# Head norms, group norm and mixing in the accumulation banks, and another order of transposes, in the attention stage of a three-block kernel

## The reference, cut to what matters

```
xn = rmsnorm(x, norm_attn);  proj = xn @ w_in            # 1024 -> 6656 columns
rq, rk, rv, rg, sq, sk, sv, ga, gb = split(proj)         # 512 512 1024 1024 512 512 512 1024 1024
rq = rope(rmsnorm(rq by 8 heads of 64, g));  rk = rope(rmsnorm(rk by heads, g)) / 8
ret = retention(rq, rk, rv)      # 8 heads of 128, two chunks of 128 tokens, decayed causal scores
ret = group_norm(ret by head, g) * silu(rg);   y_a = ret @ w_branch_ret
sq, sk = rmsnorm by heads;       sb = stick_breaking(sq, sk, sv);   y_b = sb @ w_branch_sb
x = x + (sigmoid(ga) * y_a + sigmoid(gb) * y_b) @ w_out
x = x + peer(rmsnorm(x, norm_ffn), ...)                  # and the two blocks after it
```

## Time and profile before

| | us |
|---|---|
| median of three executions | 1872.47 |
| the profiled execution's own time | 1876.42 |
| its span, first to last instruction | 1874.6 |
| busy TensorE, whole span | 1787.5 (95%) |
| busy VectorE, ScalarE, GpSimd | 1036.0, 884.3, 1089.4 |
| attention stage, up to the transposes of the next norm | 0 to about 293 |

### The profile page before, as it was taken

One profiled execution on the slowest core, in us unless ns is written; L12 is line 12 of the kernel. 1 busy time (PEld: TensorE's weight loads), 2 busy tenths in 40 slices (PEclk: granted clock), 3 DMA queues, 4 the chain that ended last, 5 costly groups with the idle time before them and its releaser, 6 DMA issues. The chain is left out here.

```text
span 1874.6 us, 36082 instructions
## 1 busy us (share of the span) xinstructions
PE 1787.5 (95%) x14238; PEld 1627.0 (87%) x14238; DVE 1036.0 (55%) x1756; ACT 884.3 (47%) x1200; POOL 1089.4 (58%) x431
## 2 busy tenths in 40 slices
PE   8799779999999999999999998999998999989998
PEld 6688669999999999888888887899997889979997
DVE  5953541597437878644444443354338863564443
ACT  5246424345543333354455455465447742345544
POOL 7764556588876666545554566565556530556563
PEclk9899889999999999999999999999999999999999
DMA  7433235255554444456567643355543411034542
GB/s 298 157 135 119 92 128 219 74 182 185 175 165 137 144 134 145 135 192 194 195 196 264 237 154 124 135 203 202 191 159 120 158 24 71 27 135 181 202 176 82
DMA packets 66178, 292.67 MB, mean 156 GB/s; under 512 B 12960, under 2 KB 13344, under 8 KB 47904
## 3 DMA queue, kind: packets, MB, share of 16 engines
q1 hardware_dynamic: 66080, 291.27, 44.6%
HBM read 289.14 MB, written 1.05 MB: 155 GB/s over the span
## 5 line engine op out<-in xcount | busy, mean ns | idle before, releaser
L2607 POOL TENSOR_TENSOR unit_lo<-unit_raw,unit_hi 128x2048 fp32r<-128x2048 f32 (+1 forms) x86 | 343.1, 4013 | 188.3 <-ACT unit_hi L1512 175.6
L2622 POOL TENSOR_TENSOR rows_lo<-rows_raw,rows_hi 128x1024 fp32r<-128x1024 f32 x128 | 308.0, 2408 | 136.7 <-ACT rows_hi L1618 85.2
L2628 POOL TENSOR_TENSOR a_lo<-table,a_hi 128x256 fp32r<-128x256 f32 x128 | 178.8, 1397 | 168.4 <-ACT a_hi L1642 168.4
L2260 DVE TENSOR_TENSOR rows_lo<-rows_raw,rows_hi 128x1024 fp32r<-128x1024 f32 x128 | 162.0, 1266 | 188.2 <-ACT rows_hi L1637 188.2
L776 PE MATMUL bank<-x_hi,rows_hi 128*128 128x256 f32 x1024 | 256.2, 288 | 1.7 <-ACT rows_hi L1600 1.7
L777 PE MATMUL bank<-x_lo,rows_hi 128*128 128x256 f32 x1024 | 250.7, 283 | 0.0
L1637 ACT ACTIVATE rows_hi<-rows_raw 128x1024 fp32r<-128x1024 f32 x128 | 135.6, 1060 | 171.0 <-PE bank L837 171.0
L2655 POOL TENSOR_TENSOR up_lo<-up_raw,up_hi 128x2048 fp32r<-128x2048 f32 x22 | 111.1, 5052 | 156.5 <-ACT up_hi L1694 126.4
L776 PEld LDWEIGHTS bank<-x_hi,rows_hi 128*128 128x128 f32 x1024 | 195.8, 191 | 1.9 <-issue 1.9
L1512 ACT ACTIVATE unit_hi<-unit_raw 128x2048 fp32r<-128x2048 f32 x71 | 135.6, 1917 | 130.8 <-PE bank L569 101.3
L777 PEld LDWEIGHTS bank<-x_lo,rows_hi 128*128 128x128 f32 x1024 | 196.1, 192 | 0.0
(11 more groups left out here) (453 smaller groups left out, 3971.0 us busy)
## 6 DMA issues: line engine op xcount, KB each, us to landing
unit_raw<-in_ring SPq DMA_DIRECT2D x75, 1024.0 KB, 4.8
rows_raw<-in_u SPq DMA_DIRECT2D x128, 512.0 KB, 3.6
rows_raw<-in_v SPq DMA_DIRECT2D x128, 512.0 KB, 4.2
up_raw<-in_up SPq DMA_DIRECT2D x44, 1024.0 KB, 5.3
down_raw<-in_down SPq DMA_DIRECT2D x22, 1024.0 KB, 4.9
const<-in_const SPq DMA_DIRECT2D x1, 1792.0 KB, 14.3
X<-in_x SPq DMA_DIRECT2D x2, 512.0 KB, 4.1
unit_raw<-in_ring SPq DMA_DIRECT2D x4, 256.0 KB, 5.4
```

The source lines that it names most:

```text
L2260: V.tensor_tensor(rows_lo[q][:, :], rows_raw[q][:, :], rows_hi_f[q % 2], ALU.subtract).then_inc(S("v_lo_ready"), 1)
L2607: return nc.gpsimd.tensor_tensor(unit_lo[SLOT_OF[n]][:, w], unit_raw[SLOT_OF[n]][:, w], hi, ALU.subtract)
L2622: nc.gpsimd.tensor_tensor(rows_lo[q][:, :], rows_raw[q][:, :], rows_hi_f[q % 2], ALU.subtract).then_inc(S("u_lo_ready"), 1)
L2628: nc.gpsimd.tensor_tensor(a_lo[q % 2][:, :], table[:, i * ROWS_RING + q, :], a_hi_f[q % 2], ALU.subtract).then_inc(S("a_lo_ready"), 1)
```

## The change

The diff below is cut: removed lines that stand in the kernel above are left out, as are the declarations. TensorE's block comes first, then ScalarE's, then VectorE's.

For slices 0, 1, 4 and 5 ScalarE now squares both banks into `tmp` and VectorE sums them. The square root takes its scale and its epsilon in the same instruction. VectorE scales, multiplies by the gain and rotates within the banks, group of tokens by group of tokens, and only the last operation writes `proj`; with it the bank is drained. ScalarE copies slices 2, 3 and 6. The group norm is made by pair of heads (`centred`, `rows_squared`, `scaled_and_gated`) while the values stand in their `ry` banks, and these banks are held out of the ring meanwhile; `ry` is drained by the last multiplication. The transposes of `Y` follow pair by pair (`retention_turned`) after slices 10, 11 and 12 and once more behind the last values of stick breaking, and `ret_hi`, `ret_lo` have a place of their own. The Sigmoid of slice 12 moves behind the last `retention_hi` on ScalarE. The mixing multiplies in the `yb` bank. Of the last transposes two banks are filled between the token groups of the second `yb`, the other two between the halves of the first `wo`.

```diff
-    ret_hi, ret_lo = x_hi, x_lo_attn
+    ret_hi, ret_lo = (view(n, ARENA_AT + TC * PROJ_W + KT * SEQ * i, [KT, SEQ], F32R) for i, n in enumerate(("ret_hi", "ret_lo")))
+    ret_junk = view("ret_junk", XN_AT + 1536, [4, DV])
...
-                        mm(outs[c][:, :], at_(x_hi_, k, c), hi[:, k, :], start=False, stop=False)
+                        mm(outs[c][:, :], at_(x_hi_, k, c), hi[:, k, :], start=half == 0 and k == 0, stop=False)
...
+                    if between and halves == 1 and c == 0:
+                        between()
...
+    def retention_turned(b):
+        o = fill(("rt", b))
+        for j in range(4):
+            h, c = 2 * b + j // 2, j % 2
+            wait_drained(pe, ("ry", h))
+            t = nc.tensor.transpose(o[:, j * P:(j + 1) * P], Y[:, c, h * DV:(h + 1) * DV], ident)
+        full(("rt", b), t)
+    def mixed_turned(banks):
+        for b in banks:
+            o = fill(("mt", b))
+            for j in range(4):
+                k, c = 2 * b + j // 2, j % 2
+                wait_drained(pe, ("yb", b // 2, c))
+                t = nc.tensor.transpose(o[:, j * P:(j + 1) * P], Y[:, c, k * P:(k + 1) * P], ident)
+            full(("mt", b), t)
...
             ret_values(2 * j - 16)
             ret_values(2 * j - 15)
+            plan.hold([("ry", h) for h in range(max(0, 2 * j - 18), 2 * j - 14)])
+        if j == N_WIN - 1:
+            plan.hold([])
...
+        if 8 <= j <= 11:
+            plan.hold([("ry", 2 * j - 16), ("ry", 2 * j - 15)])
...
+        if j >= 10:
+            retention_turned(j - 10)
...
+    retention_turned(3)
...
+        rows("ya", UNIT_AT["BRET"] + 2 * j, j, ret_hi, ret_lo, arrived=None if j else lambda k: wait_drained(pe, ("rt", k // 2)))
     for half in range(2):
         wait_drained(pe, ("sb", half))
...
+    rows("yb", UNIT_AT["BSB"], 0, sb_hi, sb_lo, halves=1)
+    rows("yb", UNIT_AT["BSB"] + 1, 1, sb_hi, sb_lo, halves=1, tokens_last=True, between=lambda: mixed_turned((0, 1)))
+    rows("wo", UNIT_AT["WOUT"], 0, mix_hi, mix_lo, arrived=lambda k: wait_drained(pe, ("mt", k // 2)), between=lambda: mixed_turned((2, 3)))
+    rows("wo", UNIT_AT["WOUT"] + 2, 1, mix_hi, mix_lo, tokens_last=True)
...
+    def gated(j):
+        for c in range(TC):
+            o = wait_filled(act, ("proj", j, c))
+            drain(("proj", j, c), A(proj[:, c, j * 512:(j + 1) * 512], o[:, :], ACT.Silu if j < 9 else ACT.Sigmoid))
+    def rows_squared(p):
+        for n in range(2):
+            h = 2 * p + n
+            act.wait_ge(S("ret_centred"), h + 1)
+            o = PS[plan.at[("ry", h)][0]]
+            for c in range(TC):
+                at_ = 400 + 2 * h + c
+                A(ret_junk[:, 2 * n + c, :], o[:, c * DV:(c + 1) * DV], ACT.Square, accum_out=stat[:, at_:at_ + 1]).then_inc(S("ret_squared"), 1)
+        act.wait_ge(S("ret_squared"), 4 * p + 4)
+        w = slice(416 + 4 * p, 420 + 4 * p)
+        A(stat[:, w], stat[:, 400 + 4 * p:404 + 4 * p], ACT.Sqrt, scale=1.0 / DV, bias=eps).then_inc(S("ret_sd"), 1)
+    def retention_hi(b):
+        hi_of(("rt", b), ret_hi[:, 2 * b:2 * b + 2, :], ("ret_group_norm", 2 * b))
...
+        if upto >= 2 and j in (0, 1, 4, 5):
+            s = (0, 1, 4, 5).index(j)
+            if s:
+                act.wait_ge(S("qk_ms"), s)
+            for c in range(TC):
+                o = wait_filled(act, ("proj", j, c))
+                A(tmp[:, 0, c * 512:(c + 1) * 512], o[:, :], ACT.Square).then_inc(S("qk_squared"), 1)
+        elif j < 7:
+            for c in range(TC):
+                copy(("proj", j, c), proj[:, c, j * 512:(j + 1) * 512])
         if upto >= 2 or 2 * j + 4 < UNIT_AT["BRET"]:
             units_ahead(2 * j + 4)
...
+        if upto >= 2 and j in (0, 1, 4, 5):
+            act.wait_ge(S("qk_ms"), s + 1)
+            A(stat[:, 128 + 16 * s:144 + 16 * s], stat[:, 64 + 16 * s:80 + 16 * s], ACT.Sqrt, scale=1.0 / DK, bias=eps).then_inc(S("qk_sd"), 1)
+        if 7 <= j < N_WIN - 1 or upto < 2 and j >= 7:
+            gated(j)
...
+        if 8 <= j <= 11:
+            rows_squared(j - 8)
+        if j >= 10:
+            retention_hi(j - 10)
...
+    retention_hi(3)
     hi_of(("sb", 1), sb_hi[:, 2:4, :])
...
+    gated(N_WIN - 1)
+    units_ahead(UNIT_AT["WOUT"] + 1)
     for b in range(4):
         hi_of(("mt", b), mix_hi[:, 2 * b:2 * b + 2, :])
+        if b == 1:
+            units_ahead(UNIT_AT["WOUT"] + 2)
...
+        j, at_ = (0, 1, 4, 5)[s], (RQ, RK, SQ, SK)[s]
+        ve.wait_ge(S("qk_squared"), 2 * s + 2)
+        sums = stat[:, 64 + 16 * s:80 + 16 * s]
+        V.tensor_reduce(sums, tmp[:, 0, :].rearrange("p (g d) -> p g d", d=DK), AX, ALU.add).then_inc(S("qk_ms"), 1)
         ve.wait_ge(S("qk_sd"), s + 1)
         rs = stat[:, 192 + 16 * s:208 + 16 * s]
...
+        step(V.reciprocal(rs, stat[:, 128 + 16 * s:144 + 16 * s]))
+        x = [wait_filled(ve, ("proj", j, c))[:, :].rearrange("p (h d) -> p h d", h=HEADS) for c in range(TC)]
+        y = [proj[:, c, at_:at_ + 512].rearrange("p (h d) -> p h d", h=HEADS) for c in range(TC)]
+        gain = bc(qk_gain[:, s, :].unsqueeze(1), [HEADS, DK])
+        for c in range(TC):
+            step.mark(V.tensor_tensor(x[c], x[c], bc(rs[:, c * HEADS:(c + 1) * HEADS].unsqueeze(2), [HEADS, DK]), ALU.mult))
+        step.sync()
         if s >= 2:
...
+            for c in range(TC):
+                drain(("proj", j, c), V.tensor_tensor(y[c], x[c], gain, ALU.mult))
             return
...
+        for c in range(TC):
+            step.mark(V.tensor_tensor(x[c], x[c], gain, ALU.mult))
+        step.sync()
         half = DK // 2
...
+        first, second = slice(0, half), slice(half, DK)
+        wave = lambda t, c: bc(t[:, c, :].unsqueeze(1), [HEADS, half])
+        part = lambda c, n: tmp[:, 1, c * 512 + n * 256:c * 512 + (n + 1) * 256].rearrange("p (h f) -> p h f", h=HEADS)
+        for n, t in enumerate((cos, sin)):
+            for c in range(TC):
+                step.mark(V.tensor_tensor(part(c, n), x[c][:, :, first], wave(t, c), ALU.mult))
         step.sync()
...
         for c in range(TC):
...
+            step.mark(V.tensor_tensor(x[c][:, :, first], x[c][:, :, second], wave(sin, c), ALU.mult))
+        step.sync()
+        for c in range(TC):
+            step.mark(V.tensor_tensor(x[c][:, :, second], x[c][:, :, second], wave(cos, c), ALU.mult))
+        for c in range(TC):
+            step.mark(V.tensor_tensor(y[c][:, :, first], part(c, 0), x[c][:, :, first], ALU.subtract))
+        step.sync()
+        for c in range(TC):
+            drain(("proj", j, c), V.tensor_tensor(y[c][:, :, second], part(c, 1), x[c][:, :, second], ALU.add))
+    if upto >= 2:
+        for s in range(4):
+            head_norm(s)
...
+    def centred(p):
+        sums = lambda h: stat[:, 384 + 2 * h:386 + 2 * h]
+        rows_of = lambda h: wait_filled(ve, ("ry", h))[:, 0:SEQ].rearrange("p (c e) -> p c e", c=TC)
+        for h in (2 * p, 2 * p + 1):
+            step.mark(V.tensor_reduce(sums(h), rows_of(h), AX, ALU.add))
+        step.sync()
+        for h in (2 * p, 2 * p + 1):
+            y = rows_of(h)
+            V.scalar_tensor_tensor(y, bc(sums(h).unsqueeze(2), [TC, DV]), -1.0 / DV, y, ALU.mult, ALU.add).then_inc(S("ret_centred"), 1)
+    def scaled_and_gated(p):
+        ve.wait_ge(S("ret_sd"), p + 1)
+        step(V.reciprocal(stat[:, 448 + 4 * p:452 + 4 * p], stat[:, 416 + 4 * p:420 + 4 * p]))
+        for h in (2 * p, 2 * p + 1):
+            o = wait_filled(ve, ("ry", h))
+            for c in range(TC):
+                wait_drained(ve, ("proj", 7 + h // 4, c))
+                w = slice(h * DV, (h + 1) * DV)
+                t = V.scalar_tensor_tensor(Y[:, c, w], o[:, c * DV:(c + 1) * DV], stat[:, 448 + 2 * h + c:449 + 2 * h + c],
+                                           proj[:, c, RG + h * DV:RG + (h + 1) * DV], ALU.mult, ALU.mult)
+            drain(("ry", h), t)
+    def retention_lo(b):
+        two = slice(2 * b, 2 * b + 2)
+        lo_of(("rt", b), ret_lo[:, two, :], ret_hi[:, two, :], ("ret_group_norm", 2 * b))
     for n in range(4):
         decayed(2 * n)
         decayed(2 * n + 1)
         if n == 1:
             stick_logits(0)
+            centred(0)
         if n == 2:
+            scaled_and_gated(0)
             stick_weights(0)
+            centred(1)
         if n == 3:
+            scaled_and_gated(1)
             stick_out(0)
             stick_logits(1)
+            centred(2)
+    scaled_and_gated(2)
+    retention_lo(0)
...
     stick_weights(1)
...
+    centred(3)
+    scaled_and_gated(3)
+    for b in (1, 2, 3):
+        retention_lo(b)
     stick_out(1)
...
+    def mixed_lo(b):
         two = slice(2 * b, 2 * b + 2)
...
+        lo_of(("mt", b), mix_lo[:, two, :], mix_hi[:, two, :])
+    gates = lambda at_, c, j: proj[:, c, at_ + j * 512:at_ + (j + 1) * 512]
+    half_rows = lambda c, j: Y[:, c, j * 512:(j + 1) * 512]
     for j in range(2):
         for c in range(TC):
+            wait_drained(ve, ("proj", 9 + j, c))
```

(49 more changed lines are left out.)

81 lines of the change are left out of this document (3 added, 78 removed).

## The result

The changed kernel took 1851.66 us (median of four executions, 1851.37 to 1853.2) against 1874.38 for the kernel before in the same session (1870.76 to 1879.43, four). The ratio is 0.9882, interval [0.9867, 0.9898], so 19 to 25 us less. A second session, 1849.44 against 1875.17, gave 0.9866 [0.9846, 0.9887]. The forecast was 1852.5 with a range of 1833 to 1865. The time was met, in part by luck: by the traces the stage gained 27 us where the sum said 20, and the median of 1872.5 that it was taken from lay 1.5 to 2.9 us under the later medians of the same kernel.

The account below looks back on a forecast made before the run. TensorE was taken as the bound, with waits and slow clock in the attention stage to win back. 46.3 us saved less 26.3 added gave net 20.0, from 1872.5 to 1852.5 us, range 1833 to 1865.

Parts of the forecast that it names:

- slow stretch: TensorE's matmuls at a lowered clock behind a wait: 2.3 us each, 1.8 more where 16 transposes come first.
- What bounds the kernel: TensorE, busy for 95% of the span; a change elsewhere pays only where TensorE stands idle or runs slow.
- Head norms: Slices before slice 8: TensorE's waits of 3.8 and 7.5 us and two slow stretches go, 15.9 us saved.
- Group norm, slices 9 to 12: New TensorE waits and slow stretches add 8.0, 4.7, 5.2 and 6.0 us; the old norm's wait going saves 15.9.
- the root's table: Norm behind the mixing: it needs its own square root table since a Sigmoid came last, 1.3 us added.
- Mixing: Additions without two SBUF operands and half the transposes moved ahead: 14.5 us saved, 1.05 added at `wo`.
- the new waits would not come: Rival, slices 9 to 12: banks come free in time or the clock holds; about 1828 us, chance 18%.
- A longer ScalarE queue: Rival: a second table load per pair and slower squares, 8 us in all; 1861 us, chance 15%.
- GpSimd would hold up in-bank operations too: Rival: scales, gains and waves still come from SBUF, so head norms slow down; 1888 us, chance 4%.

Follow-up runs that it names:

- e2: The kernel before with the new head norms alone; group norm, transposes and mixing stay old: 1861.47 us, ratio 0.9908.
- e1: The kernel before with GpSimd's split of each of the 26 projection units written as four operations of 512 columns instead of one of 2048: 1869.5 us, ratio 0.997.
- e4: The changed kernel with ScalarE's drain of slices 7 to 11 moved ahead of the second hi unit of the same turn: 1845.64 us, ratio 0.9842.
- e5: e4 with slice 12's drain also ahead of the last hi unit and the group norm's hi parts, then a dummy square root: 1836.69 us, ratio 0.9791.
- e3: The changed kernel with the old head norms put back; group norm, transposes and mixing stay new: 1865.57 us, ratio 0.9954.
- e7: The kernel before with the new head norms and the new mixing and its transposes, but the old group norm: 1843.64 us, ratio 0.9833.
- e9: e5 with VectorE's centring of pairs 0 and 2 moved into its wait for the logarithm, and pair 1's scaling ahead of the last two decays: 1828.56 us, ratio 0.9763.
- e6: The kernel before with only the mixing's product with the second gate kept in its bank and added from there: 1867.12 us, ratio 0.9958.

## Why the prediction was right, point by point

The mechanisms were right; that the number was met to 0.8 us in the first session is luck. The stage gained 27 us by the marks and not 20: in the first trace the slow stretches took 6.4 us less than charged and the waits 0.9 less. Two things hid this. The starting value of 1872.5, from three executions, was too low by 1.5 to 2.9 us, since the sessions gave 1873.97 to 1875.41 for the same kernel. And the time gained less than the stage, 22.7 us in the first session and 25.7 in the second.

**What bounds the kernel** held: what moved the time in every run was TensorE's idleness in the first 300 us and what followed it.

**Head norms** (15.9 saved): right in mechanism and size, 15.7 by the mark, shown by e2 and by e1 for the cause. A rotated slice took 10.5 us from ScalarE's first square at 25.19 to VectorE's last product, over at 35.70, under my 13. The Trainium skill, page "VectorE: DVE Perf Modes", section "Rules for kernel authors", would copy the bank to SBUF first for a chain as long as this. Here the version that copies first is the slower by 15.7 us; it also does the squares on VectorE, so not all of that is the copy's.

**Group norm, slices 9 to 12** (26.3 added with the last two terms): right in mechanism. Every predicted wait is there in the first trace. Idle us, predicted and measured: `cum 0` 2.65 and 2.08, `cum 2` 3.1 and 2.57, `sb 0` 2.35 and 2.05, `cum 4` 0.9 and 1.97, `rt 1` 2.0 and 1.54, `ya` 3.7 and 3.44, `wo` 1.05 and 1.26, the root's table 1.3 and 1.24. That is 17.05 against 16.15 (`wo` is the mixing's). That ScalarE's drains were behind three of them (`cum 2`, `rt 1`, `ya`) is shown by e4 and e5.

**The term that was mis-sized is the slow stretch.** I charged 2.3 us behind each of four new groups of waits, 9.2 in all. In the changed kernel's first trace two came. TensorE's timeline around slice 10 and at the branch product:

```profile
146.83 0.77 PE L567 MATMUL bank<-unit_hi,x_hi 128*128 128x512 f32 x1
...
151.81 1.98 PE L573 MATMUL bank<-unit_lo,x_hi 128*128 128x512 f32 x8
...
204.59 0.77 PE L567 MATMUL bank<-unit_hi,ret_hi 128*128 128x512 f32 x1 [3.44 <-issue]
...
209.70 1.98 PE L573 MATMUL bank<-unit_lo,ret_hi 128*128 128x512 f32 x8
```

The halves took 4.98 and 5.11 us against 3.63, so 1.35 and 1.48 lost; behind the waits of 2.05, 1.97 and 1.54 nothing was, which is also why `cum 4` waited longer than forecast: no slow stretch hid its chain. e5 shows the other case: there the stretch behind the wait of 2.05 was slow (from about 159.2 to 163.2) and `cum 4` waited for 1.21 us. In the second trace two of the four came as well, one of them elsewhere: the sums behind slice 11's wait took 5.29 us (3.75 in the first), after which `rt 1` had nothing to wait for, and the half at the branch product 5.32. So the term was some 3 us and not 9.2.

A slow stretch came where I had charged none, behind the 1.24 us of the root's table. TensorE there in the first trace and in the second:

```profile
267.91 1.09 PE L502 MATMUL bank<-const,XN 128*128 128x128 f32 x8 [1.65 <-DVE XN L1979]
```

```profile
266.07 1.97 PE L502 MATMUL bank<-const,XN 128*128 128x128 f32 x8 [1.65 <-DVE XN L1979]
```

From the end of that wait of 1.24 to the mark it is 11.9 us in the first trace, and 14.0 in the second, 14.1 in e3 and 14.1 in e4. So that term of 1.3 cost 3.4 us in three traces of four. The whole part was to cost 9.3 us net; by the marks it cost 2.6 to 3.3 beside what lies in shared code.

**Mixing** (14.5 saved, 1.05 left, so 13.45): about right at its place. From e2 to e7 the mark moves 17.05 us. e2 pays 8.45 and 1.87 of idleness there, 3.68 for 16 transposes and 5.52 for the half behind them (251.62 to 257.14); e7 pays 1.26, and its half takes 3.71. That is 9.1 of waits, 1.8 and 1.8, together 12.7. Another 1.4 lie behind the next norm, where the first pass of the query product took 5.34 us in e2 and 3.91 in e7, and 2.8 at slice 8 (1.6) and in slice 0 (1.2), as between e7 and the changed kernel: places that I had not counted, and the second is none of the mixing's doing.

**Rivals.** That the new waits would not come is refuted by the list of waits; its other half, that the clock holds behind waits of this length, came true behind about half of them. A longer ScalarE queue is refuted in size: four squares with their accumulator reads took 1.15 us (136.38 to 137.53), not 1.6, and no second load came. The Sigmoid follows its table load of 202.59 + 1.28 at 203.89, 0.02 us later. The rule of the Trainium skill, page "ScalarE: Activation LUTs", section "What ACT_TABLE_LOAD costs", about 1.38 us of drain on top of each load, is not borne out by that row. That GpSimd would hold up in-bank operations too is refuted by the head norm above.

## What to carry to other kernels

Beside a busy GpSimd, keep one operand of each VectorE product in an accumulation bank; a product of 512 columns took 0.65 to 0.7 us there and up to 5 with both operands in SBUF. Before holding banks longer, follow the ring by hand to the next taker of each and add up the queue of the engine that frees it: seven waits of 1.2 to 3.4 us cost as much as the 9.6 and 2.2 that they replaced and more, until the drains went ahead of work that nobody awaited. Three small moves of order (e4, e5, e9) took off another 20.9 us across sessions (1849.44 to 1828.56), nearly as much as the whole change.

## What the runs showed that I had not expected

The slow stretch behind a short wait comes and goes. The wait of 1.84 us at slice 8 stands alike in eight of the traces, behind the same matmuls. The half behind it took 5.32 to 5.34 us in five (before, changed twice, e2, e6) and 3.71 to 3.74 in three (e1, e3, e7). Behind the wait of 2.57 us the next half took 4.98 us in the changed kernel's first trace and 3.74 in its second (146.01 to 149.75). What decides it was not tried; a sum should price it as a chance of about a half and not as a toll.

Why the square in e1 found no turn between GpSimd's pieces for 17.6 us stays open. It ended at 43.28, 1.1 us after the last of the row.
